# Past keys of an attention head loaded in 128-byte runs and turned by VectorE instead of TensorE

## The chip, the core and the metric

The kernel runs on one core of a Trainium2 chip. The metric is device time in microseconds (us) of one execution, median of several runs. Before the change three runs took 1618.83, 1619.12 and 1619.57 us.

## What is computed

One inference step of a one-layer hybrid encoder: a prompt of 512 tokens and 8 sample requests of 16 tokens each (640 tokens in all, width 1024) share the weights. The layer has a combined input projection, three branches (forgetting attention, a gated linear recurrence, gated linear attention), a gated merge and an MLP. The change lies in the first branch, attention with 8 heads of 128, and there only in how the samples' past keys are brought in:

```python
def fox_attend(q, k, v, cq, ck, q_pos, k_pos):
    s = jnp.einsum('bqhd,bkhd->bhqk', q, k).astype(jnp.float32) * (FOX_HEAD_DIM ** -0.5)
    s = s + jnp.swapaxes(cq, 1, 2)[..., :, None] - jnp.swapaxes(ck, 1, 2)[..., None, :]
    s = jnp.where(k_pos[None, :] <= q_pos[:, None], s, -jnp.inf)
    p = jax.nn.softmax(s, axis=-1)
    return jnp.einsum('bhqk,bkhd->bqhd', p.astype(v.dtype), v)
# samples: k_all = concatenate([cache_fox_k, k]), 8 requests x (256 past + 16 new) keys
```

`cache_fox_k` is (1, 8, 256, 8, 128) in float32: for one head 2048 past rows of 128 numbers (512 bytes), one row every 4096 bytes, 1 MB in all. The score matmul contracts over the 128 numbers of a head, so it needs these keys with the 128 numbers on the partitions: the loaded tile has to be turned.

## The kernel before

The order of work is written out by hand for each engine; semaphores join the engines. Everything in the main part is a row of **blocks**: a block multiplies one 1024x128 slice of weights with the 640 token columns, as two halves of 24 matmuls (L530 to L544). Each weight slice arrives by DMA in one of two raw buffers (512 KB, `load`, L319 to L323), is split by ScalarE into a high part (`hi`, L1005 to L1010) and by VectorE into a low part (`lo`, L1394 to L1397); only then may TensorE start the block.

Attention is threaded into these blocks. `fox_window` (L592 on TensorE, L1081 on ScalarE, L1474 on VectorE, L370 on SyncE) does one head `a` while the three projection blocks of the next head run; there are seven such windows and an eighth whose blocks are the first merge gates. After each of the six half blocks TensorE does one unit of attention (L693 to L698); the units touched here:

- `turn_kc(j)`, L597: turns four 128x128 tiles of past keys `KC` into a PSUM bank by matmul with the identity (L606); VectorE's `kc(j)` copies the bank to `KCT` (L1481). Four of each make up a head; `turn_kc` 0 and 1 stand in the first unit, 2 and 3 in the second, where the two banks are used again.
- `scores(p)`, L620: five score tiles in the order 0, 1, samples, 2, 3; the third (p = 2) is the samples' and reads `KCT` (L640). VectorE's `soft(p)` (L1483) adds the forget terms and takes the row maximum, ScalarE's `exps(p)` the exponentials, VectorE's `norm(p)` (L1515) divides; `turn_p(p)` on TensorE (L648) waits for that (`p_normed`).
- `turn_kv(j)`, L609: turns the head's new values and keys through the same two PSUM banks, after the copies of the past keys have left them.

VectorE works in order: `lo(b+1)`, the copy to `QB`, `kc(0)`, `kc(1)`, `soft(0)`, `soft(1)`, `norm(0)`, `kc(2)`, `kc(3)`, `pt(0)`, `norm(1)`, `lo(b+2)`, `soft(2)`, `pt(1)`, `y(0)`, `norm(2)` and so on (L1529 to L1562).

All DMAs of the main part are issued by SyncE on one queue, in order. At the end of the previous head (L380) SyncE issues `load_heads` (L349), for the next head: past keys, past values (1 MB each, L346) and three rows of forget terms (L355 to L358), and behind them the weights of the window's third block, `load(b + 2)` (L382). The past keys of head 0 are loaded ahead of everything (L387). All of a head's loads count on one semaphore, `head_in` (5 transfers of 16 counts, L600, L1537).

Of the kernel before, what the change touches and what calls it, by code (L numbers as in the profile page):

```python
# [25 lines left out]
P = 128  # L26
NEG = -1.0e30
ARENA = 22600
EPS = 1e-6
FOX_HEADS, FOX_DH = 8, 128  # L30
LRU_N, CONV_W, LRU_C = 8, 4, 8.0
GLA_H, GLA_DK, GLA_DV, GLA_RANK, GLA_TAU, GLA_CH = 4, 128, 256, 16, 16.0, 64
# [62 lines left out]
def build(nc, ins, outs):  # L95
# [10 lines left out]
    NTP = TP // P  # L106
# [39 lines left out]
    with ExitStack() as ctx:  # L146
# [11 lines left out]
        TBK = bank[4:7]  # L158
# [11 lines left out]
        idf = sb("ident", [P, P])  # L170
# [44 lines left out]
        def sems(names):  # L215
            return [sem(n) for n in names.split()]
# [13 lines left out]
            "ff_ln ff_lf ff_c cp_pe cp_scan cn_pe lfn_pe lfn_sb cn_sb")  # L230

        head_in = sems("head_in0 head_in1")
        kc_turned, kc_copied, kv_turned, kv_copied, kv_stored = sems(
            "kc_turned kc_copied kv_turned kv_copied kv_stored")
        qb_ready, s_done, s_read, m_ready, p_ready, p_normed, p_turned, p_copied = sems(
            "qb_ready s_done s_read m_ready p_ready p_normed p_turned p_copied")
        o_done, y_hi, y_done, on_done, on_copied = sems("o_done y_hi y_done on_done on_copied")
# [33 lines left out]
        KC, VC = (KC0, KC1), (VC0, VC1)  # L271
        KCT, PM, QB = carve(0, (2 * NB, P), (2, NB, P), (NB, P))
# [28 lines left out]
        def diag(v):  # L301

            return bass.AP(tensor=v.tensor, offset=v.offset, ap=[v.ap[0], [P + TS_, NB], [1, TS_]])
# [14 lines left out]
        def _(sp):  # L318
# [26 lines left out]
            def load_cache(c, dst, hd, par):  # L345
                sp.dma_start(dst[:, :, :], c[0].rearrange("b (f p) h d -> p (b f) h d", p=P)[:, :, hd, :]  # L346
                             .rearrange("p f o d -> p f (o d)")).then_inc(head_in[par], 16)

            def load_heads(h, par):  # L349

                hd = h.ds() if h.terms else slice(h.c, h.c + 1)
                if h.terms or h.c > 0:
                    load_cache(cache_k, KC[par], hd, par)
                load_cache(cache_v, VC[par], hd, par)
                sp.dma_start(CB[:, par, 0:TP], nc_new[hd, 0:TP].broadcast_to((P, TP))).then_inc(head_in[par], 16)  # L355
                sp.dma_start(CB[:, par, TP:TP + PAST], nc_past[hd, :, :].rearrange("o b s -> (o b) s")
                             .unsqueeze(1).broadcast_to((NB, TS_, PAST))).then_inc(head_in[par], 16)
                sp.dma_start(CB[:, par, TP + PAST:], nc_new[hd, TP:T].broadcast_to((P, P))).then_inc(head_in[par], 16)  # L358
# [25 lines left out]

            for part in range(2):
                load(Lin(B_FOX + part), (B_FOX + part) % 2, w_fox(Lin(0), part))
            load_cache(cache_k, KC[0], slice(0, 1), 0)  # L387
            sp.wait_ge(ff_c, 1)
            sp.dma_start(nc_new, ncT[0:FOX_HEADS, :]).then_inc(scr_out, 16)
            sp.wait_ge(cp_scan, 1)  # L390
# [138 lines left out]
        def _(pe):  # L529
# [34 lines left out]
            for k in range(KT):  # L564
                mm = pe.transpose(bank[6][:, k * NR:(k + 1) * NR], vrow[0:NR, k * P:(k + 1) * P], idf[0:NR, 0:NR])
# [4 lines left out]
            for r in range(16):  # L570
                mm = pe.transpose(bank[2 + r // 4][0:FOX_HEADS, (r % 4) * P:(r % 4 + 1) * P],
                                  cp_raw[:, r * FOX_HEADS:(r + 1) * FOX_HEADS], idf[:, :])
# [5 lines left out]
            for t in range(NT):  # L578
                mm = pe.transpose(bank[6][:, t * 8:t * 8 + 8], lfT[0:FOX_HEADS, tok(t)], idf[0:FOX_HEADS, 0:FOX_HEADS])
# [3 lines left out]
            for t in range(NT):  # L583
                mm = pe.transpose(bank[7][:, t * 8:t * 8 + 8], cT[0:FOX_HEADS, tok(t)], idf[0:FOX_HEADS, 0:FOX_HEADS])
# [7 lines left out]
            def fox_window(a, par, proj):  # L592
                b = a * 3 + (B_FOX + 3)
                s = (B_FOX + 3 + par) % 2
                some = bool(a.terms) or a.c > 0

                def turn_kc(j):  # L597

                    if j == 0:
                        pe.wait_ge(head_in[par], (a.half() * 80 + 80).v)  # L600
                        if some:
                            pe.wait_ge(kv_copied, (a * 3).v)
                    if j >= 2:
                        pe.wait_ge(kc_copied, (a * 4 + (j - 1)).v)
                    for i in range(4):
                        mm = pe.transpose(TBK[j % 2][:, i * P:(i + 1) * P], KC[par][:, 4 * j + i, :], idf[:, :])  # L606
                    mm.then_inc(kc_turned, 1)

                def turn_kv(j):  # L609

                    if j < 2:
                        pe.wait_ge(kc_copied, (a * 4 + (3 + j)).v)
                    if j == 2:
                        pe.wait_ge(kv_copied, (a * 3 + 1).v)
                    for i in range(4 * j, min(4 * j + 4, 2 * NT)):
                        src = VTt if i < NT else KTt
                        mm = pe.transpose(TBK[j % 2][:, (i - 4 * j) * P:(i - 4 * j + 1) * P], src[:, par, tok(i % NT)], idf[:, :])  # L617
                    mm.then_inc(kv_turned, 1)
# [40 lines left out]
                def times_v(p):  # L659

                    t = ORD[p]
                    pe.wait_ge(p_copied, (a * 5 + (p + 1)).v)
                    pe.wait_ge(kv_copied, (a * 3 + min(p + 1, 3) if p else a * 3 + 1).v)
                    if p < 4 and (some or p > 0):
                        pe.wait_ge(y_done, (a * 5 + p).v)
                    if p == 4:
                        pe.wait_ge(s_read, (a * 5 + 4).v)
                    pt, O = PTB[:, p % 2, :], OB[p]
                    if t < NTP:
                        for i in range(t + 1):  # L670
                            mm = pe.matmul(O[:, 0:P], KVN[:, i, :], pt[:, i * P:(i + 1) * P], start=(i == 0), stop=(i == t))  # L671
                    else:
                        pe.matmul(O[:, 0:P], pt[:, 0:P], KVN[:, NTP, :], start=True, stop=False)
                        for o in range(2):
                            for f in range(2):
                                for c in range(NB // 2):
                                    i, strip = 2 * c + o, slice(2 * c * TS_, 2 * (c + 1) * TS_)
                                    mm = pe.matmul(O[strip, 0:P], PM[:, f, i, strip], VC[par][:, 2 * i + f, :], start=False,
                                                   stop=(o == 1 and f == 1))
                    mm.then_inc(o_done if t < NTP else on_done, 1)  # L680
# [6 lines left out]
                def unit(*todo):  # L687
                    def run():
                        for f, x in todo:
                            f(x)  # L690
                    return run

                u = [unit((turn_kc, 0), (turn_kc, 1), (scores, 0), (scores, 1)),  # L693
                     unit((turn_kc, 2), (turn_kc, 3), (turn_p, 0), (turn_kv, 0)),
                     unit((scores, 2), (turn_p, 1), (times_v, 0), (turn_kv, 1), (turn_kv, 2)),
                     unit((scores, 3), (turn_p, 2), (times_v, 1)),
                     unit((scores, 4), (turn_p, 3), (times_v, 2)),
# [58 lines left out]
            for n in range(LRU_N):  # L756
                mm = pe.transpose(bank[2 + n // 4][0:36, (n % 4) * P:(n % 4 + 1) * P], last[:, n, :], idf[:, :])
# [633 lines left out]
        def _(dve):  # L1391
# [82 lines left out]
            def fox_window(a, par, proj):  # L1474
                b = a * 3 + (B_FOX + 3)
                s = (B_FOX + 3 + par) % 2
                some = bool(a.terms) or a.c > 0

                def kc(j):
                    dve.wait_ge(kc_turned, (a * 4 + (j + 1)).v)  # L1480
                    dve.tensor_copy(KCT[:, 4 * j:4 * j + 4, :], TBK[j % 2].rearrange("p (t d) -> p t d", d=P)).then_inc(kc_copied, 1)  # L1481

                def soft(p):  # L1483

                    t = ORD[p]
                    w, c0 = ((t + 1) * P, 0) if t < NTP else (PAST + P, TP)
                    if p < 2:
                        if some:
                            dve.wait_ge(p_turned, (a * 5).v)
                    else:  # L1490
                        dve.wait_ge(p_turned, (a * 5 + (p - 1)).v)
                    dve.wait_ge(s_done, (a * 5 + (p + 1)).v)
                    dve.scalar_tensor_tensor(out=SP[:, p % 2, 0:w], in0=SBK[p % 2][:, 0:w], scalar=one(cn[:, t:t + 1, at(a)]),
                                             in1=CB[:, par, c0:c0 + w], op0=ALU.add, op1=ALU.add).then_inc(s_read, 1)
                    dve.wait_ge(s_read, (a * 5 + (p + 1)).v)
                    step(dve.tensor_reduce(small[:, MX, p:p + 1], SP[:, p % 2, 0:w], AX.X, ALU.max))
                    dve.tensor_scalar(small[:, NMX, p:p + 1], small[:, MX, p:p + 1], -1.0, None, ALU.mult).then_inc(m_ready, 1)  # L1497
# [34 lines left out]
                if some:  # L1532
                    dve.wait_ge(s_done, (a * 5).v)
                dve.tensor_copy(diag(QB), QT[:, par, TP:T].rearrange("p (b t) -> p b t", t=TS_)).then_inc(qb_ready, 1)
                kc(0)
                kc(1)
                dve.wait_ge(head_in[par], (a.half() * 80 + 80).v)  # L1537
                soft(0)
                soft(1)
                norm(0)  # L1540
                kc(2)
# [355 lines left out]
```

## Time and profile before

| what | value |
|---|---|
| three runs, median | 1619.12 us |
| the profiled execution, its own time | 1618.89 us |
| its span, first to last instruction | 1617.2 us |
| TensorE matmuls busy | 1545.7 us (96%) |
| VectorE, ScalarE busy | 700.6 us (43%), 616.5 us (38%) |
| attention windows | about 60 to 336 us of the span; period 34.81 us |

The profile gives busy time by engine, the chain of work that ended last, groups of instructions by line, the timeline of each engine, and the transfers. Times are us from the start of the span unless marked ns. Matmuls overlap, so that a sum of their durations exceeds the time they take; the chain counts each for the time by which it moves the chain on. SPq is the queue on which SyncE issues transfers: the time of an entry is that of issuing it, not of moving the data.

### The profile page before, as it was taken

What the parts mean: (1) busy time and instruction counts of PE and PEld (TensorE: products, weight loads), DVE (VectorE), ACT (ScalarE), POOL (GpSimd) and SP (SyncE); (2) the same over time, 40 slices, a digit from 0 to 9 for tenths busy, and PEclk for the clock granted to TensorE, in tenths of its full rate; (3) what the DMA queues carried; (4) which work ended last, traced back from release to release, by engine and by line L of the source; (5) the groups of instructions that cost most, each with busy time, mean ns of one, the idle gap of its engine ahead of it and who ended that gap; (6) DMA issues with size and microseconds to landing.
All of it is one profiled execution on the core that took longest, in us unless ns stands there. A gap on an engine that the chain in (4) does not pass through costs nothing.

```text
span 1617.2 us, 27685 instructions
## 1 busy us (share of the span) xinstructions
PE 1545.7 (96%) x10598; PEld 1486.6 (92%) x10598; DVE 700.6 (43%) x1202; ACT 616.5 (38%) x1108; POOL 25.5 (2%) x31
## 2 busy tenths in 40 slices
PE   7899999989999989999999999997899999999996
PEld 6888888889999979998898999997799999999996
DVE  7455555533268753334444433333532333333234
ACT  6233333322266752244454531234541431432522
POOL 1000000000000000000000000001100000000001
PEclk9999999999999999999999999998899999999998
DMA  4655455232222222233232222521122222222221
GB/s 138 156 140 141 122 158 151 56 95 67 80 59 65 81 62 69 82 92 100 62 107 81 78 82 78 171 69 47 39 78 78 65 77 78 76 74 70 78 79 65
DMA packets 255669, 143.40 MB, mean 89 GB/s; under 512 B 7654, under 2 KB 252071, under 8 KB 255612
## 3 DMA queue, kind: packets, MB, share of 16 engines
q1 hardware_dynamic: 255620, 142.72, 31.3%
q8 instruction: 34, 0.56, 0.1%
q14 instruction: 15, 0.12, 0.0%
HBM read 129.86 MB, written 12.84 MB: 88 GB/s over the span
## 4 chain that ended last, share of the span: by engine, by line
PE 85%; DVE 7%; ACT 4%; issue 3%; DMA 1%; DVEq 0%; ACTq 0%; POOL 0%; SPq 0%
PE psum L540 74%; PE psum L815 1%; PE psum L671 1%; PE psum L645 1%; DVE arena L1415 1%; PE psum L858 1%; DVE arena L1655 1%; ACT arena L1182 1%; DVE arena L1803 1%; PE psum L606 1%; PE psum L656 1%; PE psum L617 1%; PE psum L853 1%; PE psum L851 1%; PE psum L640 0%
## 5 line engine op out<-in xcount | busy, mean ns | idle before, releaser
L540 PE MATMUL psum<-XH,w_hi 128*128 128x320 f32 x1936 | 610.3, 315 | 5.3 <-DVE w_lo L1397 2.4
L540 PE MATMUL psum<-XH,w_lo 128*128 128x320 f32 x1936 | 599.5, 310 | 0.0
L540 PE MATMUL psum<-XL,w_hi 128*128 128x320 f32 x1936 | 599.4, 310 | 0.0
L540 PEld LDWEIGHTS psum<-XH,w_hi 128*128 128x128 f32 x1936 | 364.9, 188 | 14.7 <-DVE w_lo L1397 6.9
L540 PEld LDWEIGHTS psum<-XL,w_hi 128*128 128x128 f32 x1936 | 365.0, 189 | 0.8
L540 PEld LDWEIGHTS psum<-XH,w_lo 128*128 128x128 f32 x1936 | 364.7, 188 | 0.0
L1397 DVE TENSOR_TENSOR w_lo<-w_raw,w_hi 128x1024 fp32r<-128x1024 f32 x185 | 226.4, 1224 | 299.7 <-ACT w_hi L1010 298.8
L1010 ACT CAST w_hi<-w_raw 128x1024 fp32r<-128x1024 f32 x185 | 193.5, 1046 | 336.6 <-PE psum L540 305.7
L540 PE MATMUL psum<-YH,w_hi 128*128 128x320 f32 x1024 | 318.2, 311 | 3.0 <-DVE YL L1788 2.0
L540 PE MATMUL psum<-YL,w_hi 128*128 128x320 f32 x1024 | 317.4, 310 | 0.0
L540 PE MATMUL psum<-YH,w_lo 128*128 128x320 f32 x1024 | 317.4, 310 | 0.0
L540 PEld LDWEIGHTS psum<-YH,w_hi 128*128 128x128 f32 x1024 | 193.3, 189 | 3.9 <-issue 3.4
L540 PEld LDWEIGHTS psum<-YL,w_hi 128*128 128x128 f32 x1024 | 193.3, 189 | 0.0
L540 PEld LDWEIGHTS psum<-YH,w_lo 128*128 128x128 f32 x1024 | 193.1, 189 | 0.0
L1015 ACT ACTIVATE arena<-psum 128x320 f32<-128x320 f32 (+1 forms) x112 | 48.6, 434 | 150.0 <-PE psum L540 149.8
L1835 DVE TENSOR_TENSOR YL<-arena,YH 128x320 f32 x64 | 31.6, 493 | 147.8 <-ACT YH L1372 147.8
L1846 DVE TENSOR_TENSOR arena<-arena,psum 128x320 f32 (+1 forms) x64 | 31.2, 488 | 137.0 <-PE psum L540 137.0
L1369 ACT ACTIVATE arena<-psum 128x320 f32<-128x320 f32 x64 | 28.0, 438 | 101.1 <-PE psum L540 101.1
L1078 ACT ACTIVATE gates<-psum 128x320 f32<-128x320 f32 x48 | 20.9, 437 | 116.4 <-PE psum L540 116.3
L1581 DVE SCALAR_TENSOR_TENSOR gates<-gates,psum 128x320 f32<-128x320 f32 x48 | 23.4, 488 | 84.2 <-PE psum L540 84.2
L1099 ACT ACTIVATE arena<-arena,small 128x384 f32<-128x384 f32 (+3 forms) x40 | 23.0, 574 | 65.7 <-DVE small L1497 65.7
L556 PE MATMUL psum<-ident,arena 128*128 128x128 f32 x80 | 19.1, 417 | 25.1 <-DVE arena L1415 16.3
(229 smaller groups left out, 1204.3 us busy)
## 6 DMA issues: line engine op xcount, KB each, us to landing
w_raw<-in_w_in_dram SPq DMA_DIRECT2D x88, 512.0 KB, 3.7
w_raw<-in_w_up_dram SPq DMA_DIRECT2D x32, 512.0 KB, 4.0
w_raw<-in_w_down_dram SPq DMA_DIRECT2D x32, 512.0 KB, 3.9
w_raw<-in_w_branch_dram SPq DMA_DIRECT2D x24, 512.0 KB, 3.8
arena<-in_cache_fox_k_dram SPq DMA_DIRECT2D x8, 1024.0 KB
arena<-in_cache_fox_v_dram SPq DMA_DIRECT2D x8, 1024.0 KB
out_dram<-arena SPq DMA_DIRECT2D x16, 256.0 KB, 2.4
arena<-in_state_gla_dram SPq DMA_DIRECT2D x4, 1024.0 KB, 5.5
```

The costliest lines, as they stand in the source:

```text
L540: mm = pe.matmul(Z[h][:, 0:HT], w[s][:, k, :], x[:, k, h * HT:(h + 1) * HT], start=(k == 0 and i == 0), stop=(k == KT - 1 and i == 2))
L556: mm = pe.transpose(bk[:, k * P:(k + 1) * P], HS[:, t % 2, (4 * q + k) * P:(4 * q + k + 1) * P], idf[:, :])
L606: mm = pe.transpose(TBK[j % 2][:, i * P:(i + 1) * P], KC[par][:, 4 * j + i, :], idf[:, :])
L1010: act.copy(WH[s][:, :, :], raw[s][:, :, :]).then_inc(w_hi, 1)
L1015: act.activation(dst, Z[h][:, 0:HT], ACT.Copy, scale=scale).then_inc(z_free[h], 1)
L1078: act.activation(GT[:, s, h * HT:(h + 1) * HT], Z[h][:, 0:HT], ACT.Tanh, scale=0.5).then_inc(z_free[h], 1)
L1099: act.activation(SP[:, p % 2, 0:w], SP[:, p % 2, 0:w], ACT.Exp, bias=small[:, NMX, p:p + 1], accum_out=small[:, RSUM, p:p + 1]).then_inc(p ...
L1369: act.activation(UR[:, half], Z[h][:, 0:HT], ACT.Relu).then_inc(z_free[h], 1)
L1397: dve.tensor_tensor(WL[s][:, :, :], raw[s][:, :, :], WH[s][:, :, :].bitcast(F32), ALU.subtract).then_inc(w_lo, 1)
L1581: dve.scalar_tensor_tensor(out=g, in0=g, scalar=1.0, in1=Z[h][:, 0:HT], op0=ALU.add, op1=ALU.mult).then_inc(z_free[h], 1)
L1835: dve.tensor_tensor(YL[:, bass.ds(i * 2 + s, 1), half], UQ[:, half].unsqueeze(1), YH[:, bass.ds(i * 2 + s, 1), half].bitcast(F32), ALU.sub ...
L1846: dve.tensor_tensor(m, m, Z[h][:, 0:HT], ALU.add).then_inc(z_free[h], 1)
```

## The change

The past keys of a head are now loaded by four transfers, one for each quarter of the partitions. Quarter q holds numbers 32q to 32q+31 of every key: on a partition lie 64 runs of 32 numbers (128 bytes), from 64 groups of 32 keys. The tile is thereby already exchanged by 32x32 blocks, and VectorE's transpose, which turns each 32x32 block in place of its own, completes the turn, four 128x128 tiles by instruction, from SBUF to SBUF. TensorE's turns and the semaphore `kc_turned` go; `head_in` counts 8 transfers; VectorE waits for it ahead of `soft(0)`, which now stands ahead of `kc(0)`; TensorE waits for it only where it reads the past values.

```diff
+TB = 32
+HEAD_DMAS = 16 * 8
...
+            def load_cache_k(hd, par):
+                src = cache_k[0].rearrange("b (f p) h d -> p (b f) h d", p=TB)[:, :, hd, :].rearrange("p f o d -> p f (o d)")
+                for q in range(P // TB):
+                    sp.dma_start(KC[par][q * TB:(q + 1) * TB, :, :].rearrange("p f (a d) -> p (f a) d", d=TB),
+                                 src[:, :, q * TB:(q + 1) * TB]).then_inc(head_in[par], 16)
...
                 if h.terms or h.c > 0:
-                    load_cache(cache_k, KC[par], hd, par)
+                    load_cache_k(hd, par)
...
-            load_cache(cache_k, KC[0], slice(0, 1), 0)
+            load_cache_k(slice(0, 1), 0)
...
-                def turn_kc(j):
-
-                    if j == 0:
-                        pe.wait_ge(head_in[par], (a.half() * 80 + 80).v)
-                        if some:
-                            pe.wait_ge(kv_copied, (a * 3).v)
-                    if j >= 2:
-                        pe.wait_ge(kc_copied, (a * 4 + (j - 1)).v)
-                    for i in range(4):
-                        mm = pe.transpose(TBK[j % 2][:, i * P:(i + 1) * P], KC[par][:, 4 * j + i, :], idf[:, :])
-                    mm.then_inc(kc_turned, 1)
-
                 def turn_kv(j):
 
-                    if j < 2:
-                        pe.wait_ge(kc_copied, (a * 4 + (3 + j)).v)
+                    if j == 0 and some:
+                        pe.wait_ge(kv_copied, (a * 3).v)
...
                     pt, O = PTB[:, p % 2, :], OB[p]
+                    if t == NTP:
+                        pe.wait_ge(head_in[par], (a.half() * HEAD_DMAS + HEAD_DMAS).v)
...
-                u = [unit((turn_kc, 0), (turn_kc, 1), (scores, 0), (scores, 1)),
-                     unit((turn_kc, 2), (turn_kc, 3), (turn_p, 0), (turn_kv, 0)),
+                u = [unit((scores, 0), (scores, 1)),
+                     unit((turn_p, 0), (turn_kv, 0)),
...
                 def kc(j):
-                    dve.wait_ge(kc_turned, (a * 4 + (j + 1)).v)
-                    dve.tensor_copy(KCT[:, 4 * j:4 * j + 4, :], TBK[j % 2].rearrange("p (t d) -> p t d", d=P)).then_inc(kc_copied, 1)
+                    dve.transpose(KCT[:, 4 * j:4 * j + 4, :].rearrange("p t d -> p (t d)"),
+                                  KC[par][:, 4 * j:4 * j + 4, :].rearrange("p t d -> p (t d)")).then_inc(kc_copied, 1)
...
+                dve.wait_ge(head_in[par], (a.half() * HEAD_DMAS + HEAD_DMAS).v)
+                soft(0)
                 kc(0)
                 kc(1)
-                dve.wait_ge(head_in[par], (a.half() * 80 + 80).v)
-                soft(0)
                 soft(1)
                 norm(0)
                 kc(2)
```

## Rows read from the trace of the kernel before

**Rows 1.** The page: busy time by engine; the chain that ended last, by engine.

```profile
PE 1545.7 (96%) x10598; PEld 1486.6 (92%) x10598; DVE 700.6 (43%) x1202; ACT 616.5 (38%) x1108; POOL 25.5 (2%) x31
...
PE 85%; DVE 7%; ACT 4%; issue 3%; DMA 1%; DVEq 0%; ACTq 0%; POOL 0%; SPq 0%
```

**Rows 2.** Chain of one window (start us, us, what): first half block to third unit.

```profile
200.24 3.52 PE psum L540 x24
203.75 0.87 PE psum L606 x8
...
205.45 3.58 PE psum L540 x24
209.03 0.45 PE psum L606 x4
...
209.50 0.70 DVE arena L1481
...
210.25 0.66 PE psum L617 x4
210.90 3.52 PE psum L540 x24
...
221.22 0.34 PE psum L656 x3
...
235.05 0.58 PE psum L540 x4
```

**Rows 3.** Timeline of VectorE and ScalarE, same window (start us, us, instruction, idle before).

```profile
205.43 0.34 DVE L1493 SCALAR_TENSOR_TENSOR arena<-psum,c_nat,arena 128x128 f32<-128x128 f32 x1
...
207.58 0.29 DVE L1521 TENSOR_SCALAR arena<-arena,small 128x128 f32<-128x128 f32 x1
...
213.37 1.05 ACT L1010 CAST w_hi<-w_raw 128x1024 fp32r<-128x1024 f32 x1 [1.77 <-DMA w_raw<-in_w_in_dram]
...
216.04 0.62 DVE L1493 SCALAR_TENSOR_TENSOR arena<-psum,c_nat,arena 128x384 f32<-128x384 f32 x1 [0.37 <-PE psum L646]
...
218.88 0.42 DVE L1521 TENSOR_SCALAR arena<-arena,small 128x384 f32<-128x384 f32 x1
```

**Rows 4.** Line L1010 in the second, third and seventh windows: the third block's weights.

```profile
109.45 1.05 ACT L1010 CAST w_hi<-w_raw 128x1024 fp32r<-128x1024 f32 x1 [2.27 <-DMA w_raw<-in_w_in_dram]
...
144.53 1.05 ACT L1010 CAST w_hi<-w_raw 128x1024 fp32r<-128x1024 f32 x1 [2.56 <-DMA w_raw<-in_w_in_dram]
...
282.92 1.05 ACT L1010 CAST w_hi<-w_raw 128x1024 fp32r<-128x1024 f32 x1 [1.71 <-DMA w_raw<-in_w_in_dram]
```

**Rows 5.** SyncE's queue: head 0's past keys; then the same window (start us, us of issuing).

```profile
20.90 0.58 SPq L346 DMA_DIRECT2D arena<-in_cache_fox_k_dram  x1
...
200.42 0.37 SPq L346 DMA_DIRECT2D arena<-in_cache_fox_k_dram  x1
200.88 1.46 SPq L346 DMA_DIRECT2D arena<-in_cache_fox_v_dram  x1
202.52 3.38 SPq L355 DMA_DIRECT2D arena<-negc_new  x1
...
207.56 0.38 SPq L323 DMA_DIRECT2D w_raw<-in_w_in_dram  x1
```

**Rows 6.** Stretches; last columns are TensorE clock, DMA share, GB/s moved.

```profile
24.00:26.50 2.50, 2.50 (x11) 2.50 (x10) 1.96 (x3) 2.46 (x4) 0.00 (x0) 1.00 1.16 297
49.80:50.60 0.80, 0.80 (x8) 0.80 (x7) 0.00 (x0) 0.00 (x0) 0.00 (x0) 1.00 1.14 343
201.00:213.00 12.00, 11.76 (x86) 11.36 (x85) 6.75 (x18) 3.13 (x8) 0.00 (x0) 1.00 0.98 257
```

**Rows 7.** Transfers in 11.2 to 11.4 us: the weight columns in 32- and 64-byte runs.

```profile
DMA packets 434, 0.03 MB, mean 127 GB/s; under 512 B 433, under 2 KB 433, under 8 KB 434
```

**Rows 8.** VectorE's groups by line (busy us, mean ns of one, idle before).

```profile
L1403 DVE TENSOR_TENSOR XL<-psum,XH 128x512 fp32r<-128x512 f32 x20 | 12.9, 683 | 1.4 <-ACT XH L1022 1.4
L1481 DVE COPY arena<-psum 128x512 f32<-128x512 f32 x32 | 20.6, 686 | 20.3 <-PE psum L606 20.3
L1655 DVE TENSOR_TENSOR_SCAN arena<-arena 128x640 f32<-128x640 f32 x8 | 11.9, 1491 | 0.3
```

**Rows 9.** Chain of the last window (start us, us, what).

```profile
308.19 0.87 PE psum L606 x8
...
313.93 0.70 DVE arena L1481
```

More of the change, by code:

```diff
@@ L232, in build @@
         head_in = sems("head_in0 head_in1")
-        kc_turned, kc_copied, kv_turned, kv_copied, kv_stored = sems(
-            "kc_turned kc_copied kv_turned kv_copied kv_stored")
+        kc_copied, kv_turned, kv_copied, kv_stored = sems(
+            "kc_copied kv_turned kv_copied kv_stored")
         qb_ready, s_done, s_read, m_ready, p_ready, p_normed, p_turned, p_copied = sems(
```

## The prediction

> **What bounds the kernel now.** I read the page first. TensorE is busy 96% of the span and holds 85% of the chain that ended last [rows 1]: time goes only if TensorE has less to do or waits less. Next the chain of one attention window, from 200.24 to 235.05 us (34.81 us) [rows 2]: it runs on TensorE throughout, and the past keys show in two places. In the first unit eight turns of L606 take 0.87 us. In the second, the chain goes from TensorE's turns (0.45) to VectorE's copy L1481 (0.70) and back to the turns of L617: TensorE stands still for a PSUM bank. Then the timelines of the other engines [rows 3]: ScalarE's split of the third block's weights begins at 213.37 and had waited for their DMA. That transfer stands on SyncE's queue behind the head's loads: past keys issued at 200.42, weights at 207.56 [rows 5], and between 201 and 213 us the transfer engines are busy all the time (share 0.98) [rows 6]. So the window has a second chain, hidden just behind TensorE's: head's loads, weights, ScalarE's split, VectorE's split, softmax of the samples. The change shortens the first and lengthens the second.
>
> **The change part by part.** Times are counted from the window's start at 200.24.
>
> *TensorE's turns go.* First unit: 0.87 us of eight turns [rows 2]. Second unit: from 209.03 to 210.90 the chain now takes 1.87 us; what stays is one turn of probabilities and four of values, five at 0.87/8 = 0.109, so 0.55 us, and 1.32 go. Together 2.19 us a window.
>
> *VectorE's copies become block transposes.* No row shows a block transpose. Nearest are the copy it replaces, 686 ns for 512 columns from PSUM, and an operation of the same width, 683 ns; the dearest by column is the scan, 1491 ns for 640, that is 1.19 us for 512 [rows 8]. Below stands about half the copy, 0.35 us, if reading SBUF is quicker. I take 0.69: the result has the same 512 columns, one input. VectorE's total hardly changes, but its order does. With `soft(0)` first, it starts at about 4.1 us (scores 0 come right after the half block that ends at 3.51); from there to the end of `norm(0)` the present stretch is 205.43 to 207.87, 2.44 us [rows 3], and two transposes make it 3.8: ready at 7.9. TensorE asks for it in the second unit at 209.03 less 0.87, about 7.9 in the chain's time, some 7.6 at its queue. I put 0.3 us of waiting there: the gain of a window is 2.19 - 0.3 = 1.9 us. At 0.35 us a transpose the 0.3 goes; at 1.19 it grows by 1.0.
>
> *Waits moved.* VectorE's wait for the head's loads (ahead of `soft(0)`, with all its later work behind it) and TensorE's (ahead of the past values) cost nothing: these loads were issued a whole window earlier and are done by about 213, 25 us ahead of use. If that cover went, `lo(b+2)` and the block behind it would be late too. The wait of `turn_kv` for the copies goes with them.
>
> *The loads.* One transfer of 2048 runs of 512 bytes becomes four with 8192 runs of 128. SyncE issues three more, about 0.4 us each [rows 5]; it is held by a full queue there anyway (3.38 us for one small transfer, L355), so that costs nothing by itself. What costs is the time of the runs, since values, forget terms and weights stand behind them. Past keys alone move 297 GB/s, so 1048.6 KB take 3.53 us, 27.6 ns a run on each of 16 engines; weights with the same run length move 343 GB/s, 23.9 ns [rows 6]. The only short runs are the 32- and 64-byte columns at the start: 434 in 0.2 us, 7.4 ns each [rows 7]. No row has 128 bytes. Ends: 7.4 ns gives 3.8 us for 8192 runs, +0.3; 27.6 ns gives 14.1, +10.6. Between them, a straight line in bytes from about 55 bytes to the past keys' row gives 10.6 ns, 5.4 us, +1.9. But past keys pay 3.7 ns a run more than weights, and if every run pays that, the weights' line (10.0) plus 3.7 gives 13.7 ns, 7.0 us, +3.5. I take 13.0 ns, 6.7 us, **+3.1 us**, nearer the second: the new runs still lie 4096 bytes apart, and each transfer now ends in a quarter of the partitions, which no row shows and which can only add.
>
> A rule of the Trainium skill speaks against the change. "SBUF — State Buffer" (Door 1: the DMA port swizzle) says that 32 partitions reach only 8 of the 16 ports by which transfers write; its 189 GB/s for 1 MiB would make the keys some 5.5 us (an estimate from that page), +2.0; by that alone the sum below would be -3.1, by the value I take it is +4.6. No row of this trace shows a transfer into 32 partitions, so none agrees or disagrees.
>
> *How much of that is covered.* ScalarE's split starts 13.1 us into this window; over the six windows after the first it is 13.1 to 13.9, mean 13.4 (six rows, three shown) [rows 4]. From there to the end of `norm(2)` it is 5.9 us here (213.37 to 219.30), of which 0.37 is VectorE waiting for scores [rows 3], which will come earlier; 5.4 with what VectorE overlaps. So the probabilities are ready at about 18.9 us on average with the signal. TensorE asks for them in `turn_p(2)`, now at 221.22 [rows 2], 20.98, after the change at 20.98 - 1.9 = 19.1. The cover left is 0.2 to 0.3 us. From there every us of the loads is a us of the window:
>
> window = -1.9 + (3.1 - 0.27) = +0.93 us, seven times: +6.5.
>
> The eighth window loads no head and only gains: 0.87 and the 1.0 left of the copy's detour [rows 9], -1.9. Past keys of head 0 are issued at 20.90 us [rows 5], some 40 us ahead of the first window: nothing. Nothing else hangs on them: later units move as TensorE moves.
>
> Sum: +6.5 - 1.9 = **+4.6 us**. The profiled execution took 1618.89 us (span 1617.2, 1.7 around it), 0.23 below the median, so 1619.1 + 4.6 = 1623.7.
>
> In general the sum is 7d - 17.1, where d is what the keys' load adds; it is nought at d = 2.4 us, 12.1 ns a run.
>
> **The rivals.** *Faster: the runs are cheap.* If the keys take less than about 5.5 us, the weights still come nearly in time and the turns saved stay saved. At d = 1.9 the sum is -3.8, 1615.3; at the end of +0.3 the cover hides it and all eight windows gain 1.9: -15.2, 1603.9. For it speaks the row of short runs, whose rate is high; against it the past keys' own slower row. It decides at d = 2.4.
>
> *Much slower: quarter transfers run at half rate.* If writing into 32 partitions halves what a transfer can do, 10.6 ns become 21, the keys take 10.8 us, d = 7.3, and the sum is +34: 1653. It would show in the same wait, far longer. The skill's page above is of this kind, though by its figure the price is smaller. No row speaks for or against.
>
> *VectorE becomes the bound.* At 1.19 us the transposes make TensorE wait a us longer in the second unit, but that us then hides load time: the sum stays near +5.6. Only at three times the copy (2 us and more) would `norm(0)` and, behind `kc(2)` and `kc(3)`, `norm(1)` hold TensorE some 4 us a window: +16 and up, 1635 or more. Nothing in the rows comes near.
>
> *The change doesn't do what it says.* If the queue joined runs again, the keys would cost what they do now and 15.2 us would go, as at the cheap end. The runs of one partition lie 128 KB apart at the source, so I give this almost nothing.
>
> **How the numbers follow.** A measurement here can tell about 0.2%, 3.2 us, from no change. In terms of d: faster by over that below 2.0, slower above 2.9. Chances: the forecast, loads late by more than the cover (d from 2.4 to 5), 0.50; cheap runs 0.34; half rate or worse 0.11; VectorE 0.05. Of these, faster takes 0.25 (most of the cheap runs), same 0.27 (its rest and the lower end of the forecast), slower 0.48. The range goes from d = 1.5, 1612.5, to d = 5.3, 1639; 0.07 lie below and 0.12 above. The cases have both signs; the forecast's own range is 1619 to 1637.
>
> **What would show it.** Right: L606 gone; keys' loads 6 to 7 us instead of 3.5, packets up by about 49000; the split of the third block's weights begins 16 to 17 us into the window, waiting for its DMA; TensorE idles 2 to 3 us ahead of `turn_p(2)` (L656 before, the third unit after the second block), released by VectorE's `norm(2)`; first and second units shorter by 0.87 and 1.0; block transposes of 0.6 to 0.75 us. Wrong: a split still near 13.5 to 15, no new idle time on TensorE, and the period 1.9 us shorter; or transposes well over a us with TensorE waiting in the second unit.

## The result, and the profile after

The changed kernel takes 1643.45 us (median of 4, 1640.89 to 1645.64) against 1619.34 us of the kernel before in the same comparison: ratio 1.0147, 95% interval 1.013 to 1.0165. That is 24 us slower. The forecast was 1623.7, and its range ended at 1639. The execution profiled took 1644.32 us (span 1642.6), so between the two profiled spans lie 25.4 us.

The page first: TensorE's busy time, the chain by engine, the transfers, and the group of the turns of probabilities.

```profile
PE 1546.6 (94%) x10470; PEld 1487.5 (91%) x10470; DVE 698.2 (43%) x1202; ACT 615.6 (37%) x1108; POOL 25.5 (2%) x31
...
DMA packets 305205, 143.39 MB, mean 87 GB/s; under 512 B 73574, under 2 KB 301607, under 8 KB 305148
...
PE 76%; DVE 7%; ACT 4%; SPq 4%; issue 4%; DMA 3%; DVEq 0%; ACTq 0%; POOL 0%
...
L652 PE MATMUL psum<-ident,arena 128*128 128x128 f32 x104 | 19.9, 295 | 31.2 <-DVE arena L1519 31.2
```

The same turns and the transfers in the kernel before:

```profile
L656 PE MATMUL psum<-ident,arena 128*128 128x128 f32 x104 | 18.1, 275 | 3.3 <-DVE arena L1521 3.3
...
DMA packets 255669, 143.40 MB, mean 89 GB/s; under 512 B 7654, under 2 KB 252071, under 8 KB 255612
```

Two things stand out against [rows 1]. SyncE's queue and the DMA, which held 0% and 1% of the chain, now hold 4% and 3%, and the turns of probabilities (L652, L656 before) wait 31.2 us for `norm`, where they had waited 3.3. And TensorE has 128 matmuls fewer, yet is busy 0.9 us *longer*. A saving of work that doesn't show in the busy time means that the work left runs slower.

The chain through one window, 215.24 to 253.53 us, answers to [rows 2] (start us, us, what).

```profile
215.41 0.34 SPq L354
...
215.93 0.85 SPq L354
...
216.96 1.43 SPq L354
...
218.57 1.94 SPq L354
...
220.61 1.83 SPq L348
...
222.62 2.27 SPq L363
...
226.54 5.81 DMA w_raw<-in_w_in_dram
...
232.38 1.06 ACT w_hi L1008
...
237.44 0.43 DVE arena L1519
...
237.91 0.55 PE psum L652 x3
238.46 0.86 PE psum L669 x4
239.31 4.68 PE psum L548 x24
...
246.48 3.71 PE psum L548 x24
```

For 22.7 of the window's 38.3 us the chain is no longer on TensorE. It goes down SyncE's queue (four key transfers, the values, the forget terms), through the weights' DMA, ScalarE's split and VectorE's softmax, and returns to TensorE only at 237.91. The weights are issued 11.13 us after the keys (215.41 to 226.54), before 7.14 (200.42 to 207.56) [rows 5]: the load adds **d = 3.99 us**. The window was 34.81 us long before. Then look at the half block behind the wait: 24 matmuls in 4.68 us, while the next 24 take 3.71 as ever. In the kernel before this half block took 3.52:

```profile
222.00 3.52 PE psum L540 x24
```

TensorE's timeline shows the wait itself, and the windows view what follows it (columns from the third on: PE, PEld, DVE, ACT and POOL busy, granted clock, DMA share, GB/s).

```profile
237.91 0.55 PE L652 MATMUL psum<-ident,arena 128*128 128x128 f32 x3 [3.91 <-DVE arena L1519]
```

```profile
218.00:220.00 2.00, 2.00 (x16) 1.84 (x15) 0.75 (x4) 0.44 (x1) 0.00 (x0) 1.00 1.65 123
...
235.00:237.90 2.90, 0.00 (x0) 0.00 (x0) 2.10 (x8) 1.88 (x6) 0.00 (x0) 1.00 0.00 0
237.90:244.00 6.10, 6.09 (x32) 6.09 (x33) 2.58 (x9) 0.94 (x4) 0.00 (x0) 0.72 0.79 221
244.00:253.50 9.50, 8.52 (x84) 7.41 (x84) 4.95 (x10) 3.26 (x8) 0.00 (x0) 1.00 0.15 37
```

TensorE does nothing for 3.91 us, from 234.0 to 237.91; the second row of the windows view covers the last 2.9 of them. When it starts again it is granted 0.72 of its clock on the mean of six us (part of them at the lower of its two levels, 1.2 of 2.4 GHz), and then all of it. The first row is the keys' load: 123 GB/s.

VectorE's timeline shows the new instruction and the end of `norm(0)`, answering to [rows 3] and [rows 8].

```profile
219.96 1.29 DVE L1478 STREAM_TRANSPOSE arena<-arena 128x512 f32<-128x512 f32 x2
...
222.37 0.29 DVE L1519 TENSOR_SCALAR arena<-arena,small 128x128 f32<-128x128 f32 x1
...
233.46 1.23 DVE L1395 TENSOR_TENSOR w_lo<-w_raw,w_hi 128x1024 fp32r<-128x1024 f32 x1 [8.96 <-ACT w_hi L1008]
```

A block transpose takes 0.65 us, `norm(0)` ends 7.4 us into the window, and the split that matters waits.

### The profile page after: what moved, and what is told of

Read it like the earlier page. It is cut to its first block, busy times and chain, and to the rows that moved or that the text cites. A ratio compares the mean times of both kernels' runs of the same rounds, so it can differ in the third digit from the quotient of the medians.

```text
span 1642.6 us, 27445 instructions
## 1 busy us (share of the span) xinstructions
PE 1546.6 (94%) x10470; PEld 1487.5 (91%) x10470; DVE 698.2 (43%) x1202; ACT 615.6 (37%) x1108; POOL 25.5 (2%) x31
## 4 chain that ended last, share of the span: by engine, by line
PE 76%; DVE 7%; ACT 4%; SPq 4%; issue 4%; DMA 3%; DVEq 0%; ACTq 0%; POOL 0%
PE psum L548 67%; DMA w_raw<-in_w_in_dram 3%; SPq L354 2%; PE psum L813 1%; PE psum L669 1%; SPq L363 1%; DVE arena L1413 1%; ACT w_hi L1008 1%; PE psum L856 1%; DVE arena L1653 1%; PE psum L652 1%; ACT arena L1180 1%; SPq L348 1%; DVE arena L1801 1%; PE psum L851 1%
## 5 line engine op out<-in xcount | busy, mean ns | idle before, releaser
L548 PEld LDWEIGHTS psum<-XH,w_hi 128*128 128x128 f32 x1936 | 369.3, 191 | 13.3 <-DVE w_lo L1395 5.4
L548 PEld LDWEIGHTS psum<-XL,w_hi 128*128 128x128 f32 x1936 | 369.2, 191 | 0.8
L548 PEld LDWEIGHTS psum<-XH,w_lo 128*128 128x128 f32 x1936 | 368.6, 190 | 0.0
L1844 DVE TENSOR_TENSOR arena<-arena,psum 128x320 f32 (+1 forms) x64 | 31.2, 488 | 137.0 <-PE psum L548 137.0
L652 PE MATMUL psum<-ident,arena 128*128 128x128 f32 x104 | 19.9, 295 | 31.2 <-DVE arena L1519 31.2
L652 PEld LDWEIGHTS psum<-ident,arena 128*128 128x128 f32 x104 | 12.4, 149 | 38.0 <-DVE arena L1519 35.3
```

What stands on the lines that cost most here:

```text
L548: mm = pe.matmul(Z[h][:, 0:HT], w[s][:, k, :], x[:, k, h * HT:(h + 1) * HT], start=(k == 0 and i == 0), stop=(k == KT - 1 and i == 2))
L652: mm = pe.transpose(TBK[2][:, i * P:(i + 1) * P], SP[:, p % 2, i * P:(i + 1) * P], idf[:, :])
L1844: dve.tensor_tensor(m, m, Z[h][:, 0:HT], ALU.add).then_inc(z_free[h], 1)
```

## The experiments

The theory to test (A): the whole loss comes through the order of SyncE's queue, where the third block's weights stand behind a slower load of keys; the saving on TensorE is real. The rivals put the loss on the new instructions, or on other work that the load disturbs. Two more questions follow: what makes the load slow (the length of a run, or the 32 partitions of each transfer), and what makes half a block slow behind the wait.

**The weights go first.** In SyncE's part of the window, one line moves in front of a wait and of the head's loads:

```
                     load(b + 1, 1 - s, w_fox(a + 1, 1))
+                    load(b + 2, s, w_fox(a + 1, 2))
                     if a.terms or a.c > 0:
                         sp.wait_ge(o_done, (a * 5).v)
                     load_heads(a + 1, 1 - par)
-                    load(b + 2, s, w_fox(a + 1, 2))
```

> The changed kernel with one move: the weights of the window's third block are issued ahead of the next head's loads, not behind them. Theory A (the loss is the weights' wait behind the keys' short runs, and TensorE's clock falling after that wait): the split of the third block's weights starts 5 to 8 us into the window instead of 17, the wait ahead of turn_p(2) goes, the half block behind it takes 3.5 us again, and all eight windows keep the 1.9 us saved: 1602 to 1607 us. Theory B (the new order on VectorE or the block transposes cost the time): 1635 to 1644 us as the changed kernel.

Measured: 1602.53 us (1601.28 to 1604.17), ratio 0.9899 (0.9883 to 0.9916) to the kernel before. Its page and its chain:

```profile
PE 1530.3 (96%) x10470; PEld 1471.0 (92%) x10470; DVE 699.1 (44%) x1202; ACT 615.9 (38%) x1108; POOL 25.5 (2%) x31
```

```profile
225.38 3.52 PE psum L548 x24
...
244.15 0.34 PE psum L652 x3
244.48 0.45 PE psum L669 x4
244.93 3.52 PE psum L548 x24
...
257.97 0.15 PE psum L548
```

The chain is TensorE's again, the window lasts 32.6 us (225.38 to 257.97), 2.2 less than before, and the half block is back at 3.52. One expectation missed: the split begins 9.1 us into the window, not 5 to 8, but it no longer waits for its DMA, and TensorE no longer waits for it:

```profile
234.43 1.05 ACT L1008 CAST w_hi<-w_raw 128x1024 fp32r<-128x1024 f32 x1
```

The keys still come in short runs, but nobody waits for them. The busy time now gives the price of the clock: the same 10470 matmuls take 1530.3 us here and 1546.6 in the changed kernel, so 16.3 us of its loss are slower matmuls.

**The same move in the kernel before.**

> The kernel before with the same move alone. Theory A: the weights were in time already, so 1618 to 1620 us. If moving the weights is a gain of its own: 1605 to 1612 us.

Measured: 1619.76 us, ratio 1.0006 (0.9996 to 1.0015). The earlier weights alone are worth nothing, as the old load was still covered. So the 17 us of the run above are the change's own saving, set free.

**The changed kernel with the old load.** One transfer, 512-byte runs, all partitions; the rest stays as changed:

```
-HEAD_DMAS = 16 * 8
+HEAD_DMAS = 16 * 5
...
-                src = cache_k[0].rearrange("b (f p) h d -> p (b f) h d", p=TB)[:, :, hd, :].rearrange("p f o d -> p f (o d)")
-                for q in range(P // TB):
-                    sp.dma_start(KC[par][q * TB:(q + 1) * TB, :, :].rearrange("p f (a d) -> p (f a) d", d=TB),
-                                 src[:, :, q * TB:(q + 1) * TB]).then_inc(head_in[par], 16)
+                sp.dma_start(KC[par][:, :, :], cache_k[0].rearrange("b (f p) h d -> p (b f) h d", p=P)[:, :, hd, :]
+                             .rearrange("p f o d -> p f (o d)")).then_inc(head_in[par], 16)
```

> The changed kernel (VectorE's block transposes, no turns of the keys on TensorE) with the keys loaded as before, in one transfer of 512-byte runs to all 128 partitions; the keys then stand in the wrong order, so the past part of the attention is computed from wrong keys. Theory A (all of the loss comes through the keys' transfer, and the saved turns of 2.2 us a window are whole): 1601 to 1605 us, window period 32.6. Rival V (the block transposes on VectorE cost the window something themselves): 1608 or more.

Measured: 1605.2 us, ratio 0.9915 (0.9898 to 0.9931), a hair over the upper end of A and under the rival's 1608. The window is 32.6 us (226.55 to 259.17). The wait for `norm` is small:

```profile
L650 PE MATMUL psum<-ident,arena 128*128 128x128 f32 x104 | 18.4, 277 | 4.8 <-DVE arena L1517 4.8
```

The transposes on VectorE cost the window nothing, and with keys that arrive as before, the rest of the change is worth 13.7 us.

**The load alone in the kernel before.** The changed kernel's four transfers put into the kernel before, with its turns and copies kept.

> The kernel before with the changed load of the keys alone, TensorE's turns and the copies kept; the turns then read blocks in another order, so the past part of the attention is computed from wrong keys. The split of the third block comes 3.9 us later in its window, of which 0.27 is covered by slack; the turns of 2.2 us stand ahead of the wait and are done within it, so they cost nothing more. Theory A: each window waits as in the changed kernel, whose period it has, less what its first two units are longer by: wait 1.8 us in seven windows, 12 us, and what the clock loses behind so short a wait, 0 to 8 us: 1631 to 1641 us. Rival: the turns come on top of the load and the time is that of the changed kernel and 17 us more, 1660.

Measured: 1637.71 us (1634.19 to 1640.95), ratio 1.0105 (1.0088 to 1.0122). The window is 36.8 us (keys issued at 212.61, then 249.40, then 286.18), 2.0 more than before, and in its profile only the first two of seven windows have a slow half block (5.05 and 4.28 us). As expected by A, the turns disappear in the wait. So of two chains the load lengthens the one, the turns shorten the other, and the longer counts. With this load, taking the turns away even costs some 5 us more (1643.45 against 1637.71): TensorE then waits longer, and seven half blocks are slow instead of two.

**Short runs into all partitions.** The keys go, still in four transfers, a column block each, to all 128 partitions in 128-byte runs:

```
-                src = cache_k[0].rearrange("b (f p) h d -> p (b f) h d", p=TB)[:, :, hd, :].rearrange("p f o d -> p f (o d)")
+                src = cache_k[0].rearrange("b (f p) h d -> p (b f) h d", p=P)[:, :, hd, :].rearrange("p f o d -> p f (o d)")
...
-                    sp.dma_start(KC[par][q * TB:(q + 1) * TB, :, :].rearrange("p f (a d) -> p (f a) d", d=TB),
+                    sp.dma_start(KC[par][:, :, q * TB:(q + 1) * TB],
```

> The changed kernel with the keys in the same number of 128-byte runs in four transfers, each written to all 128 partitions instead of 32 (the keys land unexchanged, so the samples' attention is computed with wrong keys). Theory P (a transfer into 32 partitions is slow because its writes crowd): 180 to 220 GB/s in the keys' stretch, 4.8 to 5.8 us for them, split of the third block's weights 14 to 15.5 us into the window, 1608 to 1620 us. Theory R (a 128-byte run is slow wherever it goes): 120 to 145 GB/s, about 7.5 us, and 1640 to 1646 us as the changed kernel.

**Long runs into 32 partitions.** Four transfers of 32 partitions, 512-byte runs:

```
-                    sp.dma_start(KC[par][q * TB:(q + 1) * TB, :, :].rearrange("p f (a d) -> p (f a) d", d=TB),
-                                 src[:, :, q * TB:(q + 1) * TB]).then_inc(head_in[par], 16)
+                    sp.dma_start(KC[par][q * TB:(q + 1) * TB, :, :],
+                                 src[q * TB:(q + 1) * TB, :, :]).then_inc(head_in[par], 16)
```

> The changed kernel with the keys in 2048 runs of 512 bytes, in four transfers of 32 partitions (keys land unexchanged, so the samples' attention is computed with wrong keys). Theory P: slower than the 297 GB/s of the same runs into 128 partitions, 125 to 220 GB/s, keys 4.8 to 8.4 us. Theory R: 280 to 300 GB/s, 3.5 us, no wait of TensorE, 1602 to 1607 us.

Measured, one execution each: 1639.46 and 1617.59 us. SyncE's queue in one window, the short runs first, then the long ones (start us, us of issuing):

```profile
214.61 5.03 SPq L354 DMA_DIRECT2D arena<-in_cache_fox_k_dram  x4
219.73 1.36 SPq L348 DMA_DIRECT2D arena<-in_cache_fox_v_dram  x1
...
225.21 0.38 SPq L325 DMA_DIRECT2D w_raw<-in_w_in_dram  x1
```

```profile
202.20 1.93 SPq L354 DMA_DIRECT2D arena<-in_cache_fox_k_dram  x4
...
204.85 4.69 SPq L363 DMA_DIRECT2D arena<-negc_new  x1
...
211.19 0.38 SPq L325 DMA_DIRECT2D w_raw<-in_w_in_dram  x1
```

From the keys' issue to the weights' it is 10.60 us with short runs and 8.99 with long ones, that is d = 3.46 and 1.85, where the change has 3.99 and the kernel before 0. These are one window of each run; over the six windows after the first d averages 3.3, 1.7 and 3.8. Neither theory's numbers hold in full: the short runs miss R's 1640 by half a us, and the long ones take 5.4 us for the keys, as P has it, and miss R's 1602 to 1607 us. So neither is the whole cause: the length of the run is the larger part, the 32 partitions cost less than two us by themselves, and together they cost less than the sum.

**Short runs that lie together.** As with the short runs above, but from one stretch of DRAM:

```
+                src = cache_k[0, 0].rearrange("(p r) h d -> p (r h d)", p=P)
...
+                    sp.dma_start(KC[par][:, :, q * TB:(q + 1) * TB],
+                                 src[:, q * 512:(q + 1) * 512].rearrange("p (f d) -> p f d", d=TB)).then_inc(head_in[par], 16)
```

> The changed kernel with the keys read in 128-byte runs to all 128 partitions as in all_ports, but from one contiguous stretch of DRAM (8 KB a partition) in place of runs that lie 4 KB apart; the past part of the attention is computed from wrong keys. If what makes short runs dear is that they lie scattered in DRAM, the four transfers take 5 us or less and the split comes 15 us or less into the window, as with long_quarters: 1605 to 1620 us. If it is a price of each run, they take 6.5 to 7.2 us as in all_ports, the split comes at 16.6, and the time is 1635 to 1643 us.

Measured, one execution: 1636.16 us; from the keys' issue (213.67) to the weights' (224.04) 10.37 us:

```profile
213.67 4.78 SPq L354 DMA_DIRECT2D arena<-in_cache_fox_k_dram  x4
...
224.04 0.38 SPq L325 DMA_DIRECT2D w_raw<-in_w_in_dram  x1
```

d is 3.23. That the runs lie 4 KB apart is worth at most 0.23 us of 3.46 (over six windows the two runs have 3.30 and 3.33); the rest goes with the runs' number and length.

**TensorE kept at work through the wait.** Ahead of `scores(3)`, into the bank that it then overwrites:

```
+                    if p == 3 and proj:
+                        for i in range(18):
+                            pe.matmul(S[:, 0:HT], XH[:, 0, 0:P], XH[:, i % KT, 0:HT], start=True, stop=True)
```

> The changed kernel with 18 more matmuls in each of the seven windows with projections, written to the bank of scores(3) just ahead of it and overwritten by it, so that TensorE works through most of the 2.9 us in which it waited for the third block's split. Theory C (the clock: about 15 us of the 25 us lost are TensorE's granted clock falling behind that wait): the half block behind the wait is back at 3.5 us from 4.1 to 5.4, the block's wait stays, and the kernel takes 1628 to 1634 us. Theory D (what is lost is the wait alone, and the slow half blocks have another cause): half blocks stay at 4 to 5 us and the time is 1641 to 1648, no better than the changed kernel.

Measured: 1633.2 us (1631.43 to 1634.27), ratio 1.0087 (1.007 to 1.0104), 10 us *faster* than the changed kernel with 126 matmuls more. Chain and stretches of one window:

```profile
227.24 1.06 ACT w_hi L1011
...
232.78 0.55 PE psum L655 x3
233.32 0.45 PE psum L672 x4
233.77 3.52 PE psum L548 x24
```

```profile
229.00:232.78 3.78, 2.44 (x16) 1.87 (x15) 2.97 (x9) 1.89 (x6) 0.00 (x0) 1.00 0.00 0
232.78:239.00 6.22, 6.22 (x51) 5.53 (x55) 3.22 (x10) 1.37 (x5) 0.00 (x0) 1.00 0.78 225
```

The keys are issued at 210.22 and the split begins at 227.24, 17.0 us later, as in the changed kernel (215.41 and 232.38). The path from split to turn takes 5.5 us in both. The wait to fill was 3.91 us and not 2.9; 1.34 of it stay idle here. Only TensorE's idle time is filled, and all seven half blocks take 3.52 us at clock 1.00. The transfer engines move as much beside this half block as in the changed kernel (225 and 221 GB/s), so these do not make it slow. Theory C holds.

## Why the prediction was wrong

**Right: which chain takes over.** The split begins 17.0 us after the keys' issue (17.1 into the window), waiting for its DMA; TensorE stands idle 3.91 us ahead of `turn_p(2)`, released by `norm(2)`; packets rose by 49536. The chain was named in this order, and moving the weights removes the wait. Its length was named too short: 2 to 3 us, where the seven windows have 3.4 to 4.4.

**Right: what is saved.** 2.19 us a window were worked out and 2.2 appear once the weights come first (34.8 to 32.6). The 0.3 us of waiting that was taken off in the second unit does not appear, and the last window gains 2.6 us there, not 1.9 (31.16 to 28.54). With the old load, the sum's cheap end was 1603.9 and the run gave 1605.2. In that run's profile 14 matmuls of the last window took 3.34 us, where they take 1.81 once the weights come first, which is 1.5 us of it:

```profile
318.49 3.34 PE psum L667 x14
```

**Right: VectorE.** The transposes were put at 0.69 us and take 0.65; `norm(0)` was to end at 7.9 us and ends at 7.4.

**Mis-sized: the keys' load.** I took 13.0 ns a run and d = +3.1. The queue shows d = 3.99 in the window shown (215.24 to 253.53 us), so the keys take 3.53 + 3.99 = 7.5 us, 14.7 ns a run and engine (8192 runs over 16 engines are 512 each). In its steady part, 218 to 220 us, 1930 packets take 2 us, 16.6 ns each. The term "every run pays 3.7 ns, 13.7 ns" was nearly right: with 128 partitions it is 3.53 + 3.46 = 7.0 us, 13.7 ns. What I let in only as a nudge, the quarter of the partitions, brings the other 0.5 us. Over all seven windows d averages 3.82; the error of 0.7 us counts seven times, +5.0 us. A slip beside it: the break-even of d = 2.4 us is 11.7 ns a run ((3.53 + 2.44) us over 512), not 12.1.

The rule I weighed, the Trainium skill's "SBUF — State Buffer" (Door 1: the DMA port swizzle), speaks of transfers into 32 partitions. The long runs into 32 partitions bear out its figure: +1.85 us where I had worked out +2.0 from it, and 176 to 199 GB/s in that run's stretches of 1 us, from 203 to 209 us, against its 189. In this kernel the shortness of the runs was the larger part.

**Missing: the clock behind the wait.** The step "from there every us of the loads is a us of the window" failed. A wait of TensorE cost its length and, in all seven windows, a slower half block behind it: 5.06, 5.06, 4.14, 5.30, 4.68, 4.19 and 5.38 us where it should be 3.52, with the turns around it slower too. In the window shown, `turn_p(2)` comes at 22.67 us, 1.7 later than the 20.98 before, and from there to the window's end it takes 15.62 us in place of 13.83, 1.8 more. So the slower clock costs this window as much as what is left of the load's delay once the saved turns are taken off.

In the last window, for which I forecast a gain of 1.9, 1.1 was gained. The 14 matmuls of L669 took 3.34 us there, not 1.81, at a granted clock of 0.51 (357.9 to 361.3 us):

```profile
357.90 3.34 PE psum L669 x14
```

That this comes of the seven waits is not shown: the run with the old load, in which TensorE waits 0.7 us at most ahead of `turn_p(2)`, has the same 3.34.

By busy time the slow matmuls are 16.3 us, with the last window's 1.5; by the filler run 10 us in the medians and 12.9 between the profiled spans. The chain adds the whole up: over the seven windows 12.2 us more from the window's start to `turn_p(2)`, forecast 6.5; 14.3 more from there to the window's end, forecast nothing; 1.1 less in the last window, forecast 1.9. Together they are the 25.4 us between the spans. No rival contained the middle term. And the range's upper end, d = 5.3 with the clock whole, was therefore too low even for d = 3.99 once the clock fell.

The trace of the kernel before could have shown it. Its windows view, asked where TensorE has gaps, has such a stretch (the columns as above):

```profile
1100.00:1110.00 10.00, 10.00 (x71) 10.00 (x70) 2.19 (x2) 3.30 (x5) 0.00 (x0) 1.00 0.18 52
1110.00:1120.00 10.00, 6.75 (x49) 6.28 (x49) 1.99 (x5) 5.06 (x10) 0.23 (x1) 1.00 0.19 54
1120.00:1130.00 10.00, 4.51 (x24) 3.87 (x22) 7.31 (x7) 5.97 (x12) 6.77 (x3) 0.54 0.00 0
1130.00:1140.00 10.00, 5.08 (x24) 4.29 (x24) 9.86 (x12) 7.10 (x16) 2.35 (x1) 0.67 0.00 0
```

TensorE works through to 1110 us, then has gaps, and from 1120 is granted 0.54 and 0.67. I had read the clock only in rows where it was 1.00. This would have named the loss, not its size: here the gaps are of up to 4.73 us, one behind the other.

**What stays open.** Why the runs' price is what it is, and why run length and partitions together cost less than the sum, was not tried further. The short runs into all partitions also land otherwise in the tile (128 bytes every 512), so the 0.5 us between them and the changed kernel need not be the partitions' alone. Also open is why one wait lowers the clock and the next of the same length does not. What was not tried either is a wait of TensorE's without any change of the load, though the filler run, with the load as changed, leaves little else.

## What to carry to other kernels

Price a new wait of a busy TensorE with its clock as well as its length: look in the trace at hand for what it is granted behind the gaps it already has. Before a transfer is made slower, look at what stands behind it on its queue and is due first; moving those weights ahead of a load that is not due for a whole window turned 24 us lost into 17 won (1602.53 us, the best of all kernels here), while without the slower load the same move gained nothing. And a transfer has a price by the run and one by the partitions that it covers: find a row for each.

## What was not expected of the hardware

Runs of 128 bytes cost 13.2 ns (3.53 + 3.23 us over 512) to 13.7 ns each on an engine into all 128 partitions and 14.7 into 32, in the windows shown, though the 32- and 64-byte columns of [rows 7] pass at 7.4; whether they lie together in DRAM hardly matters.

The more TensorE waits, the more half blocks are slow, but not in step. In the changed kernel it waits 3.4 to 4.4 us ahead of `turn_p(2)`, and seven of seven half blocks behind are slow; with the runs that lie together 3.1 to 3.9 us, and five are; with long runs into 32 partitions 1.1 to 2.1 us, and one is, behind 1.94 us. This is how 1.38 us less of d (3.23 to 1.85) made 18.6 us between the last two runs: summed over the seven windows, 11.0 us are the load's (from the keys' issue to the weights'), and 7.7 are the clock's, the same 10470 matmuls being busy 1541.9 us in the one and 1534.2 in the other.
